# Moving the last token quarters and the gate's blocks at the start of an expert stage on one Trainium2 core

## The reference, cut to what matters

```python
def one(xb):
    q = (xb @ w_pq).reshape(PEER_BLOCK, PEER_HEADS, 2, PEER_DKH)
    s = jnp.einsum('thpd,hpkd->thpk', q, sub_keys).astype(jnp.float32)
    sv, si = lax.top_k(s, PEER_TOPK)
    ...
    best, pos = lax.top_k(cand, PEER_TOPK)
    eidx = jnp.take_along_axis(cidx, pos, axis=-1)
    g = jax.nn.softmax(best, axis=-1)
    act = jax.nn.gelu(jnp.einsum('thkd,td->thk', expert_u[eidx], xb).astype(jnp.float32), approximate=False)
    return jnp.einsum('thk,thkd->td', (g * act).astype(xb.dtype), expert_v[eidx])
```

## Time and profile before

| | us |
|---|---|
| median of 3 runs | 1369.37 (1369.22 to 1369.53) |
| the profiled execution, its own time | 1369.93 |
| its span, first to last instruction | 1368.6 |
| PE busy | 1038.9 |
| DVE busy | 877.2 |
| ACT busy | 477.8 |
| POOL busy | 293.2 |

### The profile page before, as it was taken

One profiled execution on the slowest core, in us unless ns is written; L12 is line 12 of the kernel. 1 busy time (PEld: TensorE's weight loads), 2 busy tenths in 40 slices (PEclk: granted clock), 3 DMA queues, 4 the chain that ended last, 5 costly groups with the idle time before them and its releaser, 6 DMA issues.

```text
span 1368.6 us, 16681 instructions
## 1 busy us (share of the span) xinstructions
PE 1038.9 (76%) x5827; PEld 583.6 (43%) x5827; DVE 877.2 (64%) x2219; ACT 477.8 (35%) x1321; POOL 293.2 (21%) x265
## 2 busy tenths in 40 slices
PE   7998999999999999999987887666453345443535
PEld 4776756477675646445534531322221112211201
DVE  5488643429865445855576798568777766777755
ACT  2013523101352521365357655434323332223221
POOL 0000000000000000000043444346543343433441
PEclk9999999999999999999989897877666667666656
DMA  8362454426337323145289999999999999999997
GB/s 306 132 225 93 152 217 138 184 95 239 115 123 292 117 72 127 62 144 198 101 346 426 404 427 427 424 427 425 427 426 426 426 426 425 427 425 427 425 428 297
DMA packets 56101, 391.05 MB, mean 286 GB/s; under 512 B 9931, under 2 KB 13054, under 8 KB 15954
## 3 DMA queue, kind: packets, MB, share of 16 engines
q0 software_dynamic: 37440, 268.45, 46.7%
q1 hardware_dynamic: 18578, 121.54, 24.1%
HBM read 387.87 MB, written 1.05 MB: 284 GB/s over the span
## 4 chain that ended last, share of the span: by engine, by line
DMA 21%; PE 15%; DVE 13%; ACT 5%; issue 3%; POOL 3%; another core or an unknown queue 2%; ACTq 0%; DVEq 0%
DMA e_uv<-in_experts_dram,e_listed 20%; PE bank L168 15%; DVE e_uv L2916 5%; POOL e_uv L3131 3%; ACT e_diag L229 1%; ACT m_W L229 1%; DVE e_hot L184 1%; ACT L229 1%; PE bank L173 1%; DMA m_w<-in_ada_dram 1%; DVE e_hot L2846 1%; DVE m_W L184 1%; DVE m_ctx L184 0%; ACT e_h2q L229 0%
## 5 line engine op out<-in xcount | busy, mean ns | idle before, releaser
L3131 POOL DMA_INDIRECT e_uv<-in_experts_dram,e_listed x252 | 283.5, 1125 | 1040.2 <-DVE e_listed L201 800.7
L168 PE MATMUL bank<-e_uv,e_diag 128*32 128x512 f32 x1024 | 236.6, 898 | 284.1 <-ACT e_diag L229 255.4
L2916 DVE CUSTOM_DVE_ANT_0 e_uv<-e_uv,e_h2q 128x1024 f32<-128x1024 f32 x192 | 230.2, 1223 | 107.7 <-DMA e_uv<-in_experts_dram,e_listed 95.3
L168 PEld LDWEIGHTS bank<-e_uv,e_diag 128*32 128x32 f32 x1024 | 42.0, 142 | 412.6 <-ACT e_diag L229 285.8
L168 PE MATMUL bank<-hT,weights 128*128 128x256 f32 x640 | 141.0, 380 | 2.8 <-DVE hT L190 1.4
L168 PEld LDWEIGHTS bank<-hT,weights 128*128 128x128 f32 x640 | 120.7, 190 | 21.1 <-DVE hT L190 1.6
L229 ACT ACT_TABLE_LOAD x79 | 101.4, 1283 | 6.6 <-PE bank L168 0.9
L168 PE MATMUL bank<-weights,hT 128*128 128x512 f32 (+1 forms) x256 | 101.8, 554 | 1.5 <-DVE hT L190 1.5
L229 ACT ACTIVATE e_act<-e_dot 128x4 f32<-128x4 f32 (+1 forms) x81 | 16.6, 205 | 233.0 <-DVE e_dot L2916 216.7
L196 DVE SCALAR_TENSOR_TENSOR conv<-ubuf,vec,conv 128x256 f32<-128x256 f32 x240 | 96.8, 479 | 0.6
L2916 DVE CUSTOM_DVE_ANT_0 e_uv<-e_uv,e_hT 128x1024 f32<-128x1024 f32 x64 | 76.8, 1224 | 23.0 <-DMA e_uv<-in_experts_dram,e_listed 20.6
(11 more groups left out here) (388 smaller groups left out, 1406.7 us busy)
## 6 DMA issues: line engine op xcount, KB each, us to landing
weights<-in_ada_dram SPq DMA_DIRECT2D x8, 2048.0 KB, 8.6
weights<-in_layer_out_dram SPq DMA_DIRECT2D x6, 2048.0 KB, 8.3
e_w_pq<-in_w_pq_dram SPq DMA_DIRECT2D x12, 1024.0 KB
weights<-in_layer_cmp_dram SPq DMA_DIRECT2D x4, 2048.0 KB, 8.4
weights<-in_layer_q_dram SPq DMA_DIRECT2D x2, 2048.0 KB, 8.7
weights<-in_layer_kvc_dram SPq DMA_DIRECT2D x2, 2048.0 KB, 12.5
weights<-in_layer_gb_dram SPq DMA_DIRECT2D x2, 2048.0 KB, 15.5
weights<-in_layer_ga_dram SPq DMA_DIRECT2D x2, 2048.0 KB, 15.4
```

Source lines behind the costliest of these rows:

```text
L168: ins = self.engine.matmul(out, lhsT, rhs, start=start, stop=stop, **kw)
L2916: dve.mark(c.nc.vector.tensor_tensor_reduce(u, u, h2q[tt][n], 1.0, 0.0, MUL, ADD, m["dot"][:, j:j + 1]), ("dots_set", g, c0) if n == c1 - ...
L3131: ins = c.nc.gpsimd.indirect_dma_start(out=to, out_offset=None, in_=rows, in_offset=bass.IndirectOffsetOnAxis(ap=of, axis=0))
```

## The change

Four edits of order, in three lists. On PE the two idle fillers `kept_busy` around quarter 0 are replaced by the gate's blocks 4 and 5. The quarters 2 and 3 come directly behind the first attention scores, out of the banks 2 and 3 alone, and the gate's blocks 6 and 7 follow behind them. On DVE the maximum of the first attention scores comes ahead of the second turn's `halves`. On ACT the copies of the quarters 2 and 3 come ahead of the first attention exponential and the gate's tanh.

```diff
@@ peer_tensor
     tokens_turned(0)
-    kept_busy(c, K, bank_k, 512)
+    output_gate(mix, c, (4,))
     quarter_spread(0, 0)
-    kept_busy(c, K, bank_k, 512)
+    output_gate(mix, c, (5,))
     quarter_spread(0, 1)
     queries(1)
     list_spread(0)
...
     scores(1)
     c.banks.rotate(7)
     later.att_scores(0)
-    output_gate(mix, c, range(KT // 2, KT))
-    c.banks.rotate(2, 3, 7)
+    c.banks.rotate(2, 3)
     quarter_spread(0, 2)
     quarter_spread(0, 3)
+    output_gate(mix, c, (6, 7))
+    c.banks.rotate(2, 3, 7)
@@ peer_vector
     listed(0)
+    later.att_max(0)
     halves(1)
-    later.att_max(0)
@@ peer_scalar
     folded(0)
+    quarter_set(0, 2)
+    quarter_set(0, 3)
     later.att_exp(0)
     act.wait_ge(*c.full("o", 1))
     act.f(mix["tile"][1]["o_gate"], c.banks.tile("o", 1)[:, :], ACT.Tanh, scale=0.5, tell=c.banks.emptied("o", 1))
-    quarter_set(0, 2)
-    quarter_set(0, 3)
```

## The result

| | before | changed |
|---|---|---|
| median, us | 1369.88 (14 runs) | 1371.38 (14 runs) |
| lowest to highest | 1367.62 to 1373.28 | 1370.44 to 1374.83 |
| ratio | | 1.0016, 95% interval 1.0009 to 1.0023 |
| span of the profiled execution | 1368.6 | 1369.5 |

The change made the kernel slower: by 1.5 us or 0.11% from median to median, and by 0.16% in the ratio, whose interval is 1.2 to 3.1 us. The forecast was 0.07% faster, 1368.4 us, with a range up to 1370.9. The measured median lies 0.5 us above the range and on the other side of no change, though still less than 0.2% from it. About as much lies in the base of the forecast: it was worked out from the 1369.37 us of three runs, and the kernel before is at 1369.88 over 14.

A forecast was written before the change was run, and what follows sets the result against it. The prediction took the gather stream's start and its time below 426 GB/s as the bound. 1369.93 - 1.31 + 0.3 = 1368.9 for the profiled execution, which lies 0.56 us above the median, gave 1368.4 us, range 1366.4 to 1370.9.

The forecast's parts named there:

- What bounds the kernel: Whole kernel: the gather stream's start and its time below 426 GB/s set the end; at most 3.03 us to win.
- Part 1, the fillers: PE around quarter 0: swapping two fillers for gate blocks 4 and 5 costs 0, bounds 0 and +0.3 us.
- Parts 2 and 3, the maximum and the quarters: DVE, PE and ACT before the gate's end: first dots at 696.5 against 697.0, last quarter copy 696.5 against 702.27.
- Part 4: Gate's last two blocks on PE: 2.1 us, ending at 698.0, so the fifth gather is issued 2.5 us later.
- It is hidden, by 1.4 us: Fifth gather: first bytes at 700.7, 2.7 us after issue, while earlier transfers last until about 702.1.
- The first gap closes: -1.31 us: Stream at 712 to 718 us, 333 GB/s: an earlier ninth gather restores the full rate, winning 1.31 us.
- the second gap moves as a whole: Stream at 759 to 776 us, 383 GB/s: its 1.72 us loss stays the same, only moved in time.
- +0.3: Queue about the fifth gather: being thin there costs 0.3 us, a quarter of 1.31.
- The rival of the late gate: PE's clock falls at about 694.5, fifth gather delayed, stream stands 1.1 us: +0.2 to +1.1 us; chance 0.25.

The follow-up runs named there:

- blocks_as_filler: The kernel before with only the gate's blocks 4 and 5 in place of the two fillers; ratio 1.0001 to the kernel before.
- after_again: The changed kernel once more with no edit, for a second profile; ratio 1.0021 to the kernel before.
- max_back: The changed kernel with only the maximum moved back behind the second turn's halves; ratio 1.0024 to the kernel before.
- banks_as_before: The changed kernel with banks 2, 3 and 7 taken in the kernel before's turn from the first transposed attention head on; ratio 1.0023 to the kernel before.
- after_kept: The changed kernel with zero-matrix products in PE's waits ahead of four additions of batches 2 to 5; ratio 1.0023 to the kernel before.
- after_two_fills: The changed kernel with zero-matrix products in only two of PE's waits, in batches 2 and 3; ratio 1.0006 to the kernel before.
- quarters_filled: The changed kernel with one idle product of 256 columns between quarters 2 and 3; ratio 1.0024 to the kernel before.
- before_again: The kernel before once more with no edit, for a second profile; ratio 0.9999 to the kernel before.
- before_kept: The kernel before with the same zero-matrix products in PE's waits as after_kept; ratio 1.0012 to the kernel before.
- gate_first: The changed kernel with the gate's blocks 6 and 7 ahead of quarter 2 instead of behind quarter 3; ratio 1.0000 to the kernel before.
- gate_first_again: The gate_first kernel once more with no edit; ratio 0.9998 to the kernel before.
- fifth_dots: The gate_first kernel with POOL's fifth gather made to wait for the first two dots as well; ratio 1.0013 to the kernel before.

## Why the prediction was wrong

**What bounds the kernel: right.** From 776 to 1350 us the changed kernel moves 425 GB/s. What the edits did shows in the time as what the stream lost ahead of that.

**Part 1, the fillers: right.** From the start of the queries to the first gather it is 688.28 - 683.34 = 4.94 us in the changed kernel, and in the kernel before, whose queries start at 683.83, it is 4.92. blocks_as_filler is at 1.0001. The cost was taken as 0.

**Parts 2 and 3, the maximum and the quarters: right up to PE's clock.** Quarter 2 starts at 691.06 (predicted 691.53, and the first gather is 0.47 us earlier too). The last copy ends at 696.83 (predicted 696.5).

**Part 4, the step that failed.** "Two blocks take 3.98 - 2 x 0.93 = 2.1 us, from 695.85 to 698.0." They took 3.78 us and the fifth gather went out at 700.19. The term assumed full clock, while the text itself named the fall of the clock as what it weighed most and gave the case 0.25. All six profiles with the two blocks behind unfilled quarters (changed, after_again, max_back, banks_as_before, after_kept, after_two_fills) have these blocks at 3.5 to 3.8 us and the gather 10.8 to 12.4 us behind the first, where the prediction had 698.0 - 688.75 = 9.25. It was the rule and not a chance. The first addition, predicted for 701.2, starts at 703.13 for the same reason, and the ninth gather, predicted for 704.9 to 705.0, is issued at 707.03.

"It is hidden, by 1.4 us" also fell short. The queue lasts to about 13.4 us behind the first gather (702.1 - 688.75 in the prediction's own sum), a gather at 9.87 us loses 0.1 us, and gathers at 10.8 to 11.0 us lose 0.8 to 1.3. So 3.5 us between the issue and the end of the queue were enough, and 2.4 to 2.6 us were not, where I had estimated 2.7. The stream doesn't stop at one moment either: in the changed kernel it is at 332 GB/s already from 12 to 14 us behind the first gather.

```profile
700.28:702.28 2.00, 0.00 (x0) 0.00 (x0) 1.86 (x8) 1.82 (x4) 1.70 (x2) 0.50 0.94 332
```

By the Trainium skill, TensorE: Matmul & The Clock Gate, section on HAM oscillation, a kernel with long waits for transfers between its bursts of products starts each burst at the slow clock. This case doesn't show that mechanism: PE waited only 0.34 us between the quarters, and quarters_filled has the fall without that wait.

**"The first gap closes: -1.31 us", the other step that failed.** The gap did close, 712 to 718 at 425 GB/s. Yet in before_again it isn't there at all, and neither in before_kept, while blocks_as_filler has it. The mistake was to read a loss that some executions have as a property of all. If half of them have it, closing it is worth some 0.7 us of a median, and even that can't be seen: gate_first and gate_first_again have no such gap and are at 1.0000 and 0.9998, each to about 0.001, which is 1.4 us. The same holds for "the second gap moves as a whole": it was 3.9 and 0.6 us in two profiles of one kernel.

**The sum in its terms.** I had -1.31 + 0.3 = -1.0 us. The runs put about +1.3 us for the late fifth gather (1.2 and 1.3 in two profiles) in the place of +0.3, and something between 0 and -0.7 in the place of -1.31. Together that is +0.6 to +1.3 of the measured +1.5 (1371.38 - 1369.88) or of the +2.9 of after_again beside the kernel before (1371.59 - 1368.72). The rival of the late gate had the right mechanism: the fall near 694.5 (measured 694.4), the gather at 700.5 (measured 700.19) and 1.1 us of standing stream. It ended too low, since it still subtracted the whole 1.31. Its lower end is also a slip: -1.31 + 1.1 is -0.2 and not +0.2.

**What stays open.** Up to the 1.5 to 2.9 us measured, the rest is likely the second gap, which was 3.9 us in two of the profiles with a late gate (changed, max_back) and 0.5 and 0.6 in two others. Over the profiles without zero products it was 2.1 us on average in the six with a late gate and 0.8 us in the other seven. One profile of a kernel can't tell how often. after_two_fills and the clock at 28 to 60 us support PE's clock as its cause, after_kept does not. Why PE's clock falls sooner when the quarters stand ahead of the gate is open too.

No version beat the kernel before: gate_first, the best of the changed orders, is at 1.0000 and 0.9998.

## What to carry to other kernels

Where a stream of transfers bounds a kernel, list for each issue what it waits for on the other engines, and check it with those engines at their slow clock as well: here the two blocks that released the gather took 3.5 to 3.8 us behind the quarters and 1.98 us ahead of them. Put work that releases a transfer ahead of work that only feeds another engine. And before a gap in a profile is entered as a gain, look whether a second profile of the same kernel has it; here the gaps of 1.3 and 1.7 us were 0.0 and 0.4 us in the second one.

## What the runs showed of the hardware that was not expected

- The loss follows the lateness of one gather: fifth gather 5.9 to 6.8 us behind the first, 0.0 us lost; 9.9 us, 0.1; 10.8 to 11.0 us, 0.8 to 1.3; 11.9 to 12.8 us, 1.2 to 2.0; 14.3 us, 2.7. Here 1 MB takes 2.46 us at 426 GB/s; a lead of 3.5 us was enough and one of 2.4 to 2.6 us wasn't.
- PE's clock fell while PE was busy without a pause (quarters_filled: 1.98 us for the first quarter, a filler, 3.02 us for the second). The same two quarters, put behind two blocks of the gate, ran at full clock in 3.77 us together (gate_first).
- Where PE's clock falls in the batches differs between two executions of one kernel: twice between 28 and 60 us behind the first gather in the changed kernel's first profile, and not at all in its second.
- The point where the first gather is issued lay between 688.3 and 690.6 us over the profiles, and at 688.28 and 690.20 in two profiles of the same kernel. That alone is more than the effect studied, so a profile's span does not rank two such kernels: fifth_dots has a span of 1369.4 us and the changed kernel 1369.5, at ratios of 1.0013 and 1.0016, while banks_as_before has 1368.3 at 1.0023.
